# Last output tiles of three down projections: one tile by token halves instead of two, and the next stage's weight splits moved forward

## The chip, the cores and the metric

One core of a Trainium2 chip runs the whole program. The metric is the device time of one execution in microseconds (us); the kernel before takes 2347.71 us (median of 3 runs, 2346.6 to 2347.77).

## What is computed

Two streams of 256 tokens each (the latents `x` and a context `ctx`, width 1024) go through two layers in fp32. A layer is: feed-forward 1, a mixer (convolution, mLSTM, differential attention), feed-forward 2. Each of the three adds its gated result to the stream and normalizes:

```python
def post_norm(h, delta, g, b):
    return layer_norm(ALPHA * h + delta, g, b)

def modulate(h, shift, scale):
    return h * (1.0 + scale) + shift

def swiglu(u, w_up, w_down):
    a, v = jnp.split(u @ w_up, 2, axis=-1)
    return (jax.nn.silu(a) * v) @ w_down

# feed-forward 1 of a layer; the context stream does the same with mods_c
h = post_norm(h, 0.5 * mods[2] * swiglu(modulate(h, mods[0], mods[1]), ffn1_up[l], ffn1_down[l]),
              ln_g[l, 0], ln_b[l, 0])
```

`w_down` is 2816 x 1024. In the last layer the context stream is needed only until the mixer.

## The kernel before

**Layout.** Activations lie transposed: a [128, 8, 512] tensor `h` holds 8 tiles of 128 channels, and 512 tokens on the free axis, context first (columns 0 to 255), latents second (256 to 511). Every fp32 product is made of three fp32r matmuls: weights are split into `w_hi` (rounded, by ScalarE) and `w_lo` (the rest, by VectorE), activations into `u_hi` and `u_lo` in the same way, and `chunk` (lines 1091 to 1107) issues hi x hi, hi x lo and lo x hi for each block of 128 input channels, on lines 1101, 1102 and 1103. These three lines carry most of the kernel.

**Weights.** A chunk is a [128, up to 1024] piece of weights, loaded by SyncE into one of two `raw` slots, split by ScalarE (line 1618), then by VectorE (line 2350) into one of four slots of `w_hi`/`w_lo`. `ahead(base, c, i, 8)` on both engines splits the chunk that comes four after chunk c. The raw slot can be loaded again only when VectorE has finished the split from it two chunks earlier, and a `w_hi` slot can be written only when TensorE has used what lies in it. The order of work on every engine is written out by hand; engines meet at semaphores alone.

**A down projection** (`down` on TensorE, ScalarE and VectorE) computes 8 output tiles, two in a pass of 8 chunks: chunks q = 0 to 3 make the even tile (22 blocks of input channels in all), q = 4 to 7 the odd one. The first three passes (tiles 0 to 5) use all 512 tokens in each matmul. The last pass (i = 3, tiles 6 and 7) prepares the norm. In three of the four down projections both streams are alive: norms n = 1, 3 and 4 (feed-forward 1 and 2 of layer 0, feed-forward 1 of layer 1). There `seg_order(n)` gives a first and a second half of tokens (context then latents; for n = 4 latents then context). TensorE runs tile 6 and tile 7 for the first half (132 matmuls of 256 columns, counted by `half_done`), then both again for the second half (132 more, counted by `chunk_used`, into banks `LAST_DOWN`). So tile 6's four `w_hi` slots are read until the second half. Tile 7's weights lie apart (`APART`: in `apart_hi` and in idle columns of `u_hi`), so that the four slots can take the first chunks of the next stage as soon as tile 6 lets go of them.

**The norm.** It is taken apart so that it fits beside these matmuls:
- `pivot` (TensorE, line 1127, after q = 0), `pivot_out` (ScalarE) and `centre` (VectorE, line 2527) take the mean of tiles 0 to 5 off;
- `late_branch` (VectorE, line 2558) adds a late tile from PSUM; `squares` (ScalarE, line 1734) and `add_squares` (line 2538) sum the squares, `add_rest` (line 2547) the rest of the sum. `full_tiles(n)` says up to which tile this is done for both halves at once;
- `statistics` (TensorE, lines 1138 to 1143) sums over channels; `variance`, `deviation` (ScalarE, line 1745) and `inverse` follow; `spread` (TensorE, line 1171) broadcasts the result;
- `take_mean` (line 2580) and `scaled` (line 2589) finish the norm on VectorE, `modulate` (ScalarE, lines 1690 and 1692: two instructions for each tile) makes the next stage's input in full and rounded, `low_half` (line 2500) its rest. This goes by five items: tiles 0, 1, 2-3, 4-5, 6-7.

The next stage begins with `interleaved` (TensorE, lines 1174 to 1206): four chunks side by side, tile by tile of their input, first half of tokens first. Step k needs `u_ready` of tile k. Chunks 0 and 1 start at step 0, chunk 2 at step 2, chunk 3 at step 4. After step 2 it issues the second half's `statistics`, after step 4 its `spread`, and waits there for VectorE.

Of the kernel before, what the change touches and what calls it, by code (L numbers as in the profile page):

```python
# [87 lines left out]
def is_wo(n):  # L88
    return n % 3 == 2


def seg_order(n):

    if n >= 5:
        return [LAT]
    return [LAT, CTX] if n == 4 else [CTX, LAT]
# [4 lines left out]


def full_tiles(n):
    return 4 if is_wo(n) else 6


def branch_index(n, k, order):
# [13 lines left out]
def before(n, count, first=1):  # L121

    return sum(count(m) for m in range(first, n))


def halves_done(n):

    return before(n + 1, lambda m: (4 if is_wo(m) else 8) * (len(seg_order(m)) - 1))


def sums_before(n):
# [267 lines left out]
def build(nc, x, c, ctx, c_ctx, w_ada, b_ada, ln_g, ln_b, ffn1_up, ffn1_down, ffn2_up, ffn2_down,  # L399
# [211 lines left out]
    LAST_DOWN = (4, 5)  # L611
# [402 lines left out]
    def _(pe):  # L1014
# [287 lines left out]
        def down(layer, f):  # L1302
            base, a0, d0 = BASES[layer, f"down{f}"]
            t = slice(t0_of(layer) if f else 0, TOK)
            n = 3 * layer + 2 * f + 1

            if n == DEFERRED + 1:
                pe.wait_ge(up_moved, CH_UP - 2)
            else:
                pe.wait_ge(evac_act, a0 - 1)  # L1310
                pe.wait_ge(evac_dve, d0 - 1)

            block = ADA_OF.get((layer, f"down{f}"))

            def part(q, i, cols_of, signal=chunk_used, bank=None, after_k=None, then=None):
                r = base + q + 8 * i
                ks = (LAST_K if is_apart(r) else DOWN_K)[q % 4]
                if i in PAIRED.get(n, ()):
                    paired_chunk(r, (base + q) % SPLIT, q // 4, ks, q % 4 == 0, q % 4 == 3)
                    return  # L1320
                chunk(r, (base + q) % SPLIT, q // 4 if bank is None else bank, of(g_hi, g_lo, ks, cols_of), cols_of,
                      first=(q % 4 == 0), last=(q % 4 == 3), signal=signal, after_k=after_k, then=then)

            def body(i):
                for q in range(8):
                    if isinstance(i, int) and i == 0 and q < 4:

                        pe.wait_ge(g_ready, KF * (2 * layer + f) + DOWN_K[q][-1] + 1)
                    if q % 4 == 0 and not (n == DEFERRED + 1 and isinstance(i, int) and i == 0):

                        pe.wait_ge(evac_dve, d0 - 1 + 2 * i + q // 4)
                    part(q, i, t)
                    if q == 1 and block is not None and isinstance(i, int) and 0 < i <= ADA_DOWN[layer]:
                        ada_columns(block + i - 1)
            body(0)
            body(1)
            body(2)
            i = DOWN_BODIES - 1
            segs = seg_order(n)
            pe.wait_ge(evac_dve, d0 - 1 + 2 * i)  # L1340
            if len(segs) == 2:
                for q in range(8):
                    if q == 4:
                        pe.wait_ge(evac_dve, d0 - 1 + 2 * i + 1)
                    part(q, i, segs[0][1], half_done)
                    if q == 0:
                        pivot(n)
                    if q == 1 and block is not None and i <= ADA_DOWN[layer]:
                        ada_columns(block + i - 1)
                if block is not None:  # L1350
                    pe.wait_ge(ada_ev, block + ADA_DOWN[layer])
                part(0, i, segs[1][1], bank=LAST_DOWN[0], after_k=4, then=lambda: statistics(n, 0))
                part(1, i, segs[1][1], bank=LAST_DOWN[0], after_k=3, then=lambda: spread(n, 0))
                for q in range(2, 8):
                    part(q, i, segs[1][1], bank=LAST_DOWN[q // 4])
            else:
                for q in range(4):
                    part(q, i, t)
                    if q == 0:
                        pivot(n)  # L1360
                pe.wait_ge(evac_dve, d0 - 1 + 2 * i + 1)
                for q in range(4, 8):
                    part(q, i, segs[0][1], bank=LAST_DOWN[1])
                turn_out(range(0, 6))
                last_statistics(n)
                turn_out(range(6, KD))
# [233 lines left out]
    def _(act):  # L1600
# [141 lines left out]
        def deviation(n, order):  # L1742

            act.wait_ge(ln_var, segs_before(n) + order + 1)
            act.activation(stat[:, order, 4:6], stat[:, order, 2:4], ACT.Sqrt, bias=small[:, 0:1]).then_inc(ln_std, 1)
# [66 lines left out]
        def down(layer, f):  # L1812
            base = BASES[layer, f"down{f}"][0]
# [20 lines left out]
            if not two:  # L1834
# [4 lines left out]
                scale_tiles(n, (7,))  # L1839
                deviation(n, 0)  # L1840
                return
            squares(n, (6, 7))
            if two:
                deviation(n, 0)
                ahead(base, 4, i, 8)
                modulate(n, 0, (0,))
                ahead(base, 5, i, 8)
                modulate(n, 0, (1,))
                ahead(base, 6, i, 8)
                squares(n, (6,), 1)  # L1850
                modulate(n, 0, (2, 3))
                ahead(base, 7, i, 8)
                modulate(n, 0, (4, 5))
                squares(n, (7,), 1)
                modulate(n, 0, (6,))
                deviation(n, 1)
                modulate(n, 0, (7,))
                for k in range(KD):
                    modulate(n, 1, (k,))
                    if n == 4 and k in FIRST_AFTER:  # L1860
                        proj(layer, ("mq", FIRST_AFTER.index(k)))
                if f:
                    silu_table()
# [463 lines left out]
    def _(dve):  # L2327
# [443 lines left out]
        def down(layer, f):  # L2771
# [35 lines left out]
            ahead(base, 3, i, 8, down_kn(3, two))  # L2807
            add_squares(n, (5,))
            if two:
                dve.wait_ge(half_done, halves_done(n) - 4)  # L2810
                late_branch(n, 6, 0, 0)
                add_squares(n, (6,), 0)
                dve.wait_ge(half_done, halves_done(n))
                late_branch(n, 7, 1, 0)
                add_rest(n, 7, 0)
# [4 lines left out]
                after(taken)  # L2820
                scaled(n, 0, 0)
                scaled(n, 0, 1)
                ahead(base, 4, i, 8)
                low_half(n, 0, 0)
                taken = take_mean(n, 0, 4, KD)
                ahead(base, 5, i, 8)
                low_half(n, 0, 1)
                dve.wait_ge(chunk_used, base + 8 * i + 4)
                late_branch(n, 6, LAST_DOWN[0], 1)
                scaled(n, 0, 2)  # L2830
                ahead(base, 6, i, 8)
                add_squares(n, (6,), 1)
                after(taken)
                scaled(n, 0, 3)
                low_half(n, 0, 2)
                scaled(n, 0, 4)
                ahead(base, 7, i, 8)
                low_half(n, 0, 3)
                dve.wait_ge(chunk_used, base + 8 * i + 8)
                late_branch(n, 7, LAST_DOWN[1], 1)  # L2840
                add_rest(n, 7, 1)
                add_squares(n, (7,), 1)
                variance(n, 1)
# [571 lines left out]
```

## Time and profile before

| what | value |
|---|---|
| device time, median of 3 | 2347.71 us (2346.6 to 2347.77) |
| profiled execution | span 2345.9 us, from the first to the last instruction; the runs' median is 1.8 us above it |
| TensorE busy | 2324.3 us (99%), 12926 matmuls |
| VectorE busy | 1658.6 us (71%) |
| ScalarE busy | 1034.5 us (44%) |
| DMA | 356.89 MB, mean 152 GB/s |

A matmul's own duration in the profile covers its run through the array, and matmuls overlap, so the time that one costs in a stream is the distance from its start to the next one's. An engine's idle time counts only where TensorE later waits for it.

### The profile page before, as it was taken

The page shows a single profiled execution, that of the slowest core. Times are in us where ns is not written, and L with a number is a line of the kernel's source. Part 1 is how long each engine was busy: PE and PEld are TensorE (multiplying, and loading weights), DVE is VectorE, ACT ScalarE, POOL GpSimd, SP SyncE. Part 2 cuts the span into 40 slices and gives each one's busy share as a digit, 9 for nine tenths or more (in the row PEclk, how much of TensorE's full clock was granted, in tenths as well). Part 3 has the DMA queues.
Part 4 walks back from the last instruction along what each step waited for, and adds up shares of the span by engine and source line. Part 5 has one row for each costly group of instructions (what it writes and reads, how often), then busy time and mean ns, then how long its engine had stood idle before and what let it go on. Part 6 is the DMA issues. An engine that isn't in the chain of part 4 may idle for free.

```text
span 2345.9 us, 35713 instructions
## 1 busy us (share of the span) xinstructions
PE 2324.3 (99%) x12926; PEld 2024.5 (86%) x12926; DVE 1658.6 (71%) x2777; ACT 1034.5 (44%) x1765; POOL 194.4 (8%) x186
## 2 busy tenths in 40 slices
PE   8999999999999999999999999999999999999998
PEld 6888889888888888898888898888898898999997
DVE  6998577457757655669885368886665757878876
ACT  5423224435556544363222264322245347756554
POOL 2111000000000000021120000111100000001220
PEclk9999999999999999999999999999999999999999
DMA  8788465232222322338783328776544433656654
GB/s 276 241 249 246 127 213 149 82 95 76 73 68 81 95 81 70 110 91 254 237 246 113 94 80 249 232 237 181 180 117 117 117 99 103 172 143 196 193 160 141
DMA packets 540057, 356.89 MB, mean 152 GB/s; under 512 B 15206, under 2 KB 490896, under 8 KB 539920
## 3 DMA queue, kind: packets, MB, share of 16 engines
q1 hardware_dynamic: 538472, 354.70, 51.6%
q8 instruction: 84, 1.38, 0.3%
q10 hardware_dynamic: 1448, 0.38, 0.1%
q14 instruction: 53, 0.43, 0.1%
HBM read 337.20 MB, written 17.83 MB: 151 GB/s over the span
## 4 chain that ended last, share of the span: by engine, by line
PE 94%; DVE 2%; ACT 1%; issue 1%; DMA 1%; POOL 0%; DVEq 0%; SPq 0%; ACTq 0%; POOLq 0%
PE ps L1101 25%; PE ps L1103 25%; PE ps L1102 25%; PE ps L1401 2%; PE ps L1402 2%; PE ps L1400 2%; PE ps L1114 1%; PE ps L1475 1%; PE ps L1193 1%; PE ps L1195 1%; PE ps L1194 1%; PE ps L1512 1%; PE ps L1116 1%; DVE w_lo L2350 0%; PE ps L1413 0%
## 5 line engine op out<-in xcount | busy, mean ns | idle before, releaser
L1618 ACT ACTIVATE w_hi<-raw 128x1024 fp32r<-128x1024 f32 (+3 forms) x430 | 423.3, 985 | 848.9 <-PE ps L1103 661.1
L2350 DVE TENSOR_TENSOR w_lo<-raw,w_hi 128x1024 fp32r<-128x1024 f32 (+3 forms) x430 | 495.0, 1152 | 423.1 <-ACT w_hi L1618 417.6
L1101 PE MATMUL ps<-u_hi,w_hi 128*128 128x512 f32 (+2 forms) x2176 | 778.1, 358 | 1.1 <-DVE w_lo L2350 0.7
L1103 PE MATMUL ps<-u_hi,w_lo 128*128 128x512 f32 (+2 forms) x2176 | 773.5, 355 | 0.0
L1102 PE MATMUL ps<-u_lo,w_hi 128*128 128x512 f32 (+2 forms) x2176 | 773.1, 355 | 0.0
L1101 PEld LDWEIGHTS ps<-u_hi,w_hi 128*128 128x128 f32 x2176 | 411.2, 189 | 60.1 <-issue 1.3
L1103 PEld LDWEIGHTS ps<-u_hi,w_lo 128*128 128x128 f32 x2176 | 411.1, 189 | 57.7
L1102 PEld LDWEIGHTS ps<-u_lo,w_hi 128*128 128x128 f32 x2176 | 411.4, 189 | 55.8
L2768 DVE SCALAR_TENSOR_TENSOR ada_acc<-ada_in_up,cs,ada_acc 128x512 f32<-128x512 f32 x378 | 284.2, 813 | 0.0
L1101 PE MATMUL ps<-g,w_hi 128*128 128x512 f32 (+1 forms) x572 | 206.9, 362 | 0.0
L1102 PE MATMUL ps<-g,w_hi 128*128 128x512 f32 (+1 forms) x572 | 204.1, 357 | 0.0
L1103 PE MATMUL ps<-g,w_lo 128*128 128x512 f32 (+1 forms) x572 | 204.1, 357 | 0.0
L2282 POOL TENSOR_TENSOR fold<-fold 128x512 f32<-128x512 f32 x64 | 87.6, 1368 | 880.3 <-DMA fold<-fold_out 877.8
L1802 ACT ACTIVATE g<-scr 128x512 f32 (+1 forms) x66 | 41.8, 633 | 200.9 <-DVE scr L2678 192.1
L1101 PEld LDWEIGHTS ps<-g,w_hi 128*128 128x128 f32 x572 | 108.1, 189 | 16.8 <-DVE w_lo L2350 0.5
L1102 PEld LDWEIGHTS ps<-g,w_hi 128*128 128x128 f32 x572 | 108.1, 189 | 16.1 <-issue 0.7
L1103 PEld LDWEIGHTS ps<-g,w_lo 128*128 128x128 f32 x572 | 108.1, 189 | 15.5
L2350 DVE TENSOR_TENSOR w_lo<-h,w_hi 128x1024 fp32r<-128x1024 f32 (+2 forms) x66 | 71.6, 1087 | 18.9 <-ACT w_hi L1618 18.5
L2260 POOL TENSOR_TENSOR scr<-h 128x256 f32<-128x256 f32 x3 | 3.7, 1227 | 972.5 <-DVE h L2558 972.5
L1618 ACT ACTIVATE w_hi<-h 128x1024 fp32r<-128x1024 f32 (+2 forms) x66 | 62.0, 942 | 40.2 <-PE ps L1103 30.0
L1402 PE MATMUL ps<-w_lo,u_hi 128*128 128x512 f32 x192 | 74.8, 389 | 0.0
L1400 PE MATMUL ps<-w_hi,u_hi 128*128 128x512 f32 x192 | 74.8, 389 | 0.0
(394 smaller groups left out, 3678.0 us busy)
## 6 DMA issues: line engine op xcount, KB each, us to landing
raw<-in_ffn_up SPq DMA_DIRECT2D x150, 512.0 KB, 4.8
raw<-in_w_in SPq DMA_DIRECT2D x132, 512.0 KB, 3.8
ada_in_up<-in_w_ada SPq DMA_DIRECT2D x108, 512.0 KB, 4.6
raw<-in_ffn_down SPq DMA_DIRECT2D x67, 384.0 KB, 3.6
fold_out<-ada_acc SPq DMA_DIRECT2D x32, 512.0 KB, 3.5
fold<-fold_out SPq DMA_DIRECT2D x32, 512.0 KB, 5.4
raw<-in_ffn_down SPq DMA_DIRECT2D x42, 320.0 KB, 3.2
h<-in_ffn_up SPq DMA_DIRECT2D x22, 512.0 KB, 4.0
```

Source lines behind the costliest of these rows:

```text
L1101: pe.matmul(ps[bank][:, cols_of], wh, a_hi, start=a, stop=False)
L1102: pe.matmul(ps[bank][:, cols_of], wh, a_lo, start=False, stop=False)
L1103: m = pe.matmul(ps[bank][:, cols_of], wl, a_hi, start=False, stop=b)
L1114: pe.matmul(ps[bank][:, :].rearrange("p (s t) -> p s t", s=2), wh, g[:, :, k, SEG:TOK], start=(first and n == 0), stop=False)
L1400: pe.matmul(ps[t][:, :], u_hi[:, k, own], wh, start=(k == 0), stop=False)
L1401: pe.matmul(ps[t][:, :], u_lo[:, k, own], wh, start=False, stop=False)
L1402: m = pe.matmul(ps[t][:, :], u_hi[:, k, own], wl, start=False, stop=(k == KD - 1))
L1618: act.activation(hi, whole, ACT.Copy).then_inc(hi_done, 1)
L1802: act.activation(g_hi[:, 2 * i + q // 2, t0:TOK], scr[2 + q // 2][:, t0:TOK], ACT.Copy).then_inc(g_hi_done, 1)
L2282: pool.tensor_tensor(fold[:, 0:n, :], fold[:, 0:n, :], fold[:, n:2 * n, :], ALU.add).then_inc(fold_half, 1)
L2350: dve.tensor_tensor(lo, whole, hi.bitcast(F32), ALU.subtract).then_inc(lo_done, 1)
L2768: dve.scalar_tensor_tensor(ada_acc[:, s, :], w, by, ada_acc[:, s, :], ALU.mult, ALU.add).then_inc(ada_mul, 1)
```

## The change

Tile 6 is now computed for all tokens at once, like tiles 0 to 5; only tile 7 is done by halves. `full_tiles` of a down projection goes from 6 to 7, so tile 6's evacuation, squares and sums are done once for 512 columns. The first half's `statistics` and `spread` move from the second half of tile 6 to the second half of tile 7. The splits of the next stage's first four chunks (`ahead(base, 4..7, i, 8)`) move forward in the order of ScalarE and VectorE.

```diff
 def full_tiles(n):
-    return 4 if is_wo(n) else 6
+    return 4 if is_wo(n) else 7
...
-    return before(n + 1, lambda m: (4 if is_wo(m) else 8) * (len(seg_order(m)) - 1))
+    return before(n + 1, lambda m: 4 * (len(seg_order(m)) - 1))
...
                 for q in range(8):
                     if q == 4:
                         pe.wait_ge(evac_dve, d0 - 1 + 2 * i + 1)
-                    part(q, i, segs[0][1], half_done)
+                    if q < 4:
+                        part(q, i, t)
+                    else:
+                        part(q, i, segs[0][1], half_done)
...
-                part(0, i, segs[1][1], bank=LAST_DOWN[0], after_k=4, then=lambda: statistics(n, 0))
-                part(1, i, segs[1][1], bank=LAST_DOWN[0], after_k=3, then=lambda: spread(n, 0))
-                for q in range(2, 8):
-                    part(q, i, segs[1][1], bank=LAST_DOWN[q // 4])
+                part(4, i, segs[1][1], bank=LAST_DOWN[1])
+                part(5, i, segs[1][1], bank=LAST_DOWN[1], after_k=0, then=lambda: statistics(n, 0))
+                part(6, i, segs[1][1], bank=LAST_DOWN[1], after_k=1, then=lambda: spread(n, 0))
+                part(7, i, segs[1][1], bank=LAST_DOWN[1])
...
-            squares(n, (6, 7))
             if two:
+                ahead(base, 4, i, 8)
+                squares(n, (6,))
+                ahead(base, 5, i, 8)
+                squares(n, (7,))
                 deviation(n, 0)
-                ahead(base, 4, i, 8)
-                modulate(n, 0, (0,))
-                ahead(base, 5, i, 8)
-                modulate(n, 0, (1,))
                 ahead(base, 6, i, 8)
-                squares(n, (6,), 1)
+                modulate(n, 0, (0, 1))
+                ahead(base, 7, i, 8)
                 modulate(n, 0, (2, 3))
-                ahead(base, 7, i, 8)
+                squares(n, (7,), 1)
                 modulate(n, 0, (4, 5))
-                squares(n, (7,), 1)
-                modulate(n, 0, (6,))
                 deviation(n, 1)
-                modulate(n, 0, (7,))
+                modulate(n, 0, (6, 7))
...
             if two:
-                dve.wait_ge(half_done, halves_done(n) - 4)
+                dve.wait_ge(chunk_used, base + 8 * i + 4)
                 late_branch(n, 6, 0, 0)
+                ahead(base, 4, i, 8)
                 add_squares(n, (6,), 0)
+                ahead(base, 5, i, 8)
                 dve.wait_ge(half_done, halves_done(n))
                 late_branch(n, 7, 1, 0)
...
                 scaled(n, 0, 0)
                 scaled(n, 0, 1)
-                ahead(base, 4, i, 8)
+                ahead(base, 6, i, 8)
                 low_half(n, 0, 0)
                 taken = take_mean(n, 0, 4, KD)
-                ahead(base, 5, i, 8)
+                scaled(n, 0, 2)
                 low_half(n, 0, 1)
-                dve.wait_ge(chunk_used, base + 8 * i + 4)
-                late_branch(n, 6, LAST_DOWN[0], 1)
-                scaled(n, 0, 2)
-                ahead(base, 6, i, 8)
-                add_squares(n, (6,), 1)
+                ahead(base, 7, i, 8)
                 after(taken)
                 scaled(n, 0, 3)
                 low_half(n, 0, 2)
                 scaled(n, 0, 4)
-                ahead(base, 7, i, 8)
-                low_half(n, 0, 3)
                 dve.wait_ge(chunk_used, base + 8 * i + 8)
                 late_branch(n, 7, LAST_DOWN[1], 1)
+                low_half(n, 0, 3)
                 add_rest(n, 7, 1)
```

VectorE between the first half's spread and the second half's sums, in the kernel before (L2589 scales a tile or two, L2350 splits a chunk of the next stage, L2500 is the low half of the next input, L2580 takes the mean off, L2558 adds a late tile, L2538 adds squares):

```order
L2589 TENSOR_TENSOR h<-h,ps 128x256 x2
L2350 TENSOR_TENSOR w_lo<-raw,w_hi 128x1024
L2500 TENSOR_TENSOR u_lo<-scr_82,u_hi 128x256
L2580 TENSOR_TENSOR h<-h,ps 128x4x256
L2350 TENSOR_TENSOR w_lo<-raw,w_hi 128x1024
L2500 TENSOR_TENSOR u_lo<-scr_82,u_hi 128x256
L2558 SCALAR_TENSOR_TENSOR h<-ps,gate,h 128x256
L2589 TENSOR_TENSOR h<-h,ps 128x2x256
L2350 TENSOR_TENSOR w_lo<-raw,w_hi 128x1024
L2538 TENSOR_TENSOR scr_80<-scr_80,scr_79 128x256
```

The same place in the changed kernel (each line number is one higher):

```order
L2590 TENSOR_TENSOR h<-h,ps 128x256 x2
L2351 TENSOR_TENSOR w_lo<-raw,w_hi 128x1024
L2501 TENSOR_TENSOR u_lo<-scr_82,u_hi 128x256
L2581 TENSOR_TENSOR h<-h,ps 128x4x256
L2590 TENSOR_TENSOR h<-h,ps 128x2x256
L2501 TENSOR_TENSOR u_lo<-scr_82,u_hi 128x256
L2351 TENSOR_TENSOR w_lo<-raw,w_hi 128x1024
L2590 TENSOR_TENSOR h<-h,ps 128x2x256
L2501 TENSOR_TENSOR u_lo<-scr_78,u_hi 128x2x256
L2590 TENSOR_TENSOR h<-h,ps 128x2x256
L2559 SCALAR_TENSOR_TENSOR h<-ps,gate,h 128x256
L2501 TENSOR_TENSOR u_lo<-scr_82,u_hi 128x2x256
```

Two of the four splits and the second half's share of tile 6 are gone from here. What follows is the second half's L2548 and L2539 (sum and squares of tile 7), which now stand behind the low half of tiles 4-5.

ScalarE around the second half's square of tile 7 (L1734), before (L1690 and L1692 are the two instructions of `modulate`, here for tiles 4, 5 and 6, L1618 is a split):

```order
L1618 ACTIVATE w_hi<-raw 128x1024
L1690 ACTIVATE scr_82<-h,mod_b,mod_a 128x256
L1692 ACTIVATE u_hi<-h,mod_b,mod_a 128x256
L1690 ACTIVATE scr_82<-h,mod_b,mod_a 128x256
L1692 ACTIVATE u_hi<-h,mod_b,mod_a 128x256
L1734 ACTIVATE scr_79<-h 128x256
L1690 ACTIVATE scr_78<-h,mod_b,mod_a 128x256
```

And in the changed kernel (tiles 3, 4 and 5; L1737 is the square):

```order
L1693 ACTIVATE scr_78<-h,mod_b,mod_a 128x256
L1695 ACTIVATE u_hi<-h,mod_b,mod_a 128x256
L1737 ACTIVATE scr_79<-h 128x256
L1693 ACTIVATE scr_82<-h,mod_b,mod_a 128x256
L1695 ACTIVATE u_hi<-h,mod_b,mod_a 128x256
L1693 ACTIVATE scr_82<-h,mod_b,mod_a 128x256
L1695 ACTIVATE u_hi<-h,mod_b,mod_a 128x256
```

The square of tile 7 now stands ahead of tiles 4 and 5, so ScalarE waits for VectorE's L2559 before it begins them.

## Rows read from the trace of the kernel before

**Rows 1.** The page, busy time of each engine: us, share of the span, instructions.
```profile
PE 2324.3 (99%) x12926; PEld 2024.5 (86%) x12926; DVE 1658.6 (71%) x2777; ACT 1034.5 (44%) x1765; POOL 194.4 (8%) x186
```

**Rows 2.** Timeline of PE, n = 3: start us, duration us, line; 512 columns, 60 steps.
```profile
1335.62 0.39 PE L1101 MATMUL ps<-g,w_hi 128*128 128x512 f32 x1
...
1349.22 0.28 PE L1101 MATMUL ps<-g,w_hi 128*128 128x256 f32 x1
```

**Rows 3.** Timeline of PE, n = 3: pivot, then 126 steps of 256 columns.
```profile
1351.38 1.02 PE L1127 MATMUL ps<-scr,con 128*128 128x512 f32 x2
1351.84 0.68 PE L1101 MATMUL ps<-g,w_hi 128*128 128x256 f32 x1
...
1352.47 0.28 PE L1103 MATMUL ps<-g,w_lo 128*128 128x256 f32 x1
...
1367.59 0.28 PE L1103 MATMUL ps<-g,w_lo 128*128 128x256 f32 x1
```

**Rows 4.** Timeline of PE, n = 3: first statistics, first spread.
```profile
1367.70 0.50 PE L1138 MATMUL ps<-con,scr 128*128 128x1 f32 x4
...
1370.82 0.60 PE L1171 MATMUL ps<-con,stat 128*128 128x128 f32 x4
```

**Rows 5.** Timeline of PE, n = 3: next stage's first matmul, second statistics.
```profile
1383.49 0.28 PE L1193 MATMUL ps<-u_hi,w_hi 128*128 128x256 f32 x1
...
1386.01 0.50 PE L1138 MATMUL ps<-con,scr 128*128 128x1 f32 x4
```

**Rows 6.** Timeline of DVE, n = 3, after the first spread.
```profile
1371.53 0.75 DVE L2589 TENSOR_TENSOR h<-h,ps 128x256 f32<-128x256 f32 x2 [0.62 <-PE ps L1171]
1372.20 1.22 DVE L2350 TENSOR_TENSOR w_lo<-raw,w_hi 128x1024 fp32r<-128x1024 f32 x1
1373.33 0.42 DVE L2500 TENSOR_TENSOR u_lo<-scr,u_hi 128x256 fp32r<-128x256 f32 x1
1373.67 1.22 DVE L2580 TENSOR_TENSOR h<-h,ps 128x1024 f32<-128x1024 f32 x1
...
1375.93 0.42 DVE L2500 TENSOR_TENSOR u_lo<-scr,u_hi 128x256 fp32r<-128x256 f32 x1
1376.27 0.48 DVE L2558 SCALAR_TENSOR_TENSOR h<-ps,gate,h 128x256 f32<-128x256 f32 x1
1376.66 0.68 DVE L2589 TENSOR_TENSOR h<-h,ps 128x512 f32<-128x512 f32 x1
...
1380.57 0.69 DVE L2500 TENSOR_TENSOR u_lo<-scr,u_hi 128x512 fp32r<-128x512 f32 x1
```

**Rows 7.** Timeline of DVE, n = 3: tile 7 of the second half, its sum and squares.
```profile
1384.10 0.48 DVE L2558 SCALAR_TENSOR_TENSOR h<-ps,gate,h 128x256 f32<-128x256 f32 x1
1384.61 0.42 DVE L2547 TENSOR_TENSOR scr<-h 128x256 f32<-128x256 f32 x1
1385.06 0.42 DVE L2538 TENSOR_TENSOR scr<-scr,scr 128x256 f32<-128x256 f32 x1
```

**Rows 8.** Timeline of ACT, n = 3: modulation of two tiles, then the square.
```profile
1381.39 0.59 ACT L1690 ACTIVATE scr<-h,mod_b,mod_a 128x256 f32<-128x256 f32 x1
1381.88 0.59 ACT L1692 ACTIVATE u_hi<-h,mod_b,mod_a 128x256 fp32r<-128x256 f32 x1
...
1384.61 0.42 ACT L1734 ACTIVATE scr<-h 128x256 f32<-128x256 f32 x1 [1.15 <-DVE h L2558]
```

**Rows 9.** Timeline of PE, n = 1: a wait in the last pass, and the matmul before it.
```profile
385.83 0.28 PE L1103 MATMUL ps<-g,u_lo 128*128 128x256 f32 x1
386.52 0.39 PE L1101 MATMUL ps<-g,u_hi 128*128 128x256 f32 x1 [0.41 <-DVE u_lo L2350]
```

**Rows 10.** Windows of PE at the kernel's end: us, PE busy (instructions), granted clock, DMA.
```profile
2336.50:2337.50 1.00, 1.00 (x9) 1.00 0.00 0
2337.60:2340.30 2.70, 0.00 (x0) 1.00 0.00 0
2340.50:2342.50 2.00, 0.00 (x0) 0.50 0.35 131
```

## The prediction

> **What bounds the kernel now.** The page's first part comes first: TensorE (PE in rows) is busy for 2324.3 of 2345.9 us, 99% [rows 1]. VectorE (DVE) at 71% and ScalarE (ACT) at 44% have room on average, so every us that the change moves counts only through TensorE: matmul time saved, or a wait of TensorE that was not there. The next view is the timeline of TensorE in the last pass of a down projection. I work in the stage of n = 3, where nothing else goes on, and count t from the first matmul of that pass, 1349.22 us [rows 2]. Statistics start at t = 18.48 and the spread at 21.60 [rows 4], the next stage's first matmul at 34.27 and the second statistics at 36.79 [rows 5], all with no wait of TensorE. That they have none is a matter of cover: between the first spread and the next stage TensorE has 12.7 us of matmuls, under which the first half's normalizing is done. The timelines of DVE and ACT [rows 6 to 8] show how long that work is. VectorE's low half of tile 0 is there at t = 24.5, that of tile 1 at 27.1, that of tiles 2-3 at 32.0 [rows 6], where TensorE wants them at 34.3, 35.0 and 35.7.
>
> **What is taken off TensorE.** Tile 6 takes 66 matmuls of 512 columns in place of 132 of 256. A step of 512 columns is (1349.22 - 1335.62) / 60 = 0.2267 us [rows 2], one of 256 is (1367.59 - 1352.47) / 126 = 0.120 us [rows 3]. That is 66 x (0.240 - 0.2267) = 0.88 us for a stage, 2.6 us for the three. The Trainium skill, in "TensorE: Matmul & The Clock Gate", section "Back-to-back issue gap", gives N / 2.4 + 2.5 ns for a lone matmul of N columns at the full clock; by that a pair of 256 costs only 2.5 ns more than one of 512, and the gain would be 0.2 us a stage. The rows decide, with 13 ns.
> In n = 1 TensorE also waits 0.41 us for a split of tile 7's weights [rows 9]. The first half of tile 7 now starts some 7 us later (66 x 0.2267 against 66 x 0.12), so this wait goes, with the late restart after it: 0.5 us.
>
> **What the change moves.** It halves the cover. Of the second half's matmuls only tile 7's 66 are left, and the first half's statistics and spread stand inside them. Step by step, in t:
> - tile 6 whole 14.96, plus the pivot's 0.86 (from 1351.38 to 1352.47 less two steps [rows 3]): 15.82. The first half of tile 7, 7.92: 23.74.
> - 21 matmuls, 2.52: statistics at 26.26. They cost 1.32 (3.12 between the rows less 15 steps) [rows 4]. VectorE has added tile 7 and its squares by then: it needs three instructions and a square, 1.7 us.
> - 21 matmuls more: spread at 30.10, which costs 0.43. 24 matmuls are left, 2.88: the next stage at 33.41, where 34.27 was. Cover after the spread: 3.3 us instead of 12.7.
> VectorE starts `scaled` 0.71 us after the spread does [rows 4, 6], at 30.81. With the starts of neighbouring rows as the length of each [rows 6]:
> - two small `scaled` 0.67, a split 1.13, low half of tile 0: done at 33.03, 0.4 before TensorE needs it. No wait, just.
> - mean off tiles 4 to 7 1.13, `scaled` of tiles 2-3 0.60, low half of tile 1: done at 35.1. TensorE wants it at 33.41 + 6 x 0.12 = 34.13: **1.0 us** of wait.
> - a split 1.13, `scaled` of 4-5 0.60, low half of tiles 2-3 0.69: done at 37.55, ScalarE's four instructions for them (0.49 each [rows 8]) being ready at 36.9. TensorE has step 1 done at 36.0: **1.6 us**.
> - TensorE's step 2 (9 matmuls) ends at 38.85, and it comes to the second half's statistics. These need VectorE's evacuation, sum and squares of tile 7, at 1384.10 to 1385.48 in rows 7, which before were done 0.5 us ahead of TensorE. Now the evacuation starts at 38.1, behind `scaled` of 6-7. Behind it the new order crosses the two engines: ScalarE's square of tile 7 stands ahead of its modulation of tiles 4 and 5, and VectorE's low half of 4-5 stands ahead of the sum and the squares. So the chain is evacuation 0.48, square 0.42, four modulations 2.0, low half 0.69, sum 0.35, squares 0.42: done at 42.4. **3.6 us**, the largest wait.
> A wait also makes TensorE's restart late: the first matmul after one lasts 0.39 instead of 0.28 us [rows 9]; I put 0.15 for each of the three. Sum of the waits: 1.0 + 1.6 + 3.6 + 0.45 = 6.65 us.
> Behind the statistics ScalarE does the deviation and then four modulations of tiles 6 and 7 (before, two of them were behind); the second half's mean and scaling come some 1 us later against TensorE. In n = 1 and 3 the second half of the interleaved chunks, in n = 4 the projection's next splits, wait for them. The trace has no row for that; nothing is the lower bound, 1.1 us (this delay and a restart) the upper, and I take 0.8, since these chains have less than a us to spare.
> The four early splits cost nothing: two now stand where VectorE waits for TensorE's half of tile 7 (t = 16 to 24), the cover being that wait. They do not repay the cost, since no wait of TensorE for a next-stage split is there to be removed in n = 3.
> Tile 6 done once saves VectorE and ScalarE an instruction or two, in the stretch before t = 16, where nothing is late. The last down projection (n = 6) has one half only and keeps its order.
>
> **The sum.** n = 3: 6.65 + 0.8 - 0.88 = 6.6 us. n = 4: the same. n = 1: 6.6 - 0.5 = 6.1. Together 19.3 us, 0.8%. The profiled execution's span is 2345.9 us, and the median of the runs stands 1.8 above a span; 2347.7 + 19.3 = **2367 us**. About 0.2% (4.7 us) is what a measurement of this kernel can tell from no change.
>
> **The rivals.**
> *The clock falls too.* TensorE's granted clock is full (2.4 GHz) for the whole working part. At the end TensorE is idle from about 2337.5; until 2340.3 the clock is still full, from 2340.5 on it is half (1.2 GHz) [rows 10]. So some 2.9 us of idleness brought it down, and my third wait has 3.6, with two short ones just before. Against: before that end TensorE had only small matmuls, in my stage it is dense. Were it to fall in each stage for some 5 us of dense matmuls, each would lose 2.5 us: 2367 + 7.5 = 2374.5 us. Below, a fall that ends with the wait costs nothing. The Trainium skill's page named above, section "What's actually happening", calls the lower clock the state of an idle engine, which activity releases; by that rule too a long wait is paid for twice. Chance 30%.
> *Only the early waits cost.* If the crossed chain is shorter than I make it, by ScalarE getting to the square sooner or TensorE being later there, the third wait shrinks by 2.5 us: 2367 - 7.5 = 2359.5 us. For it: 3.6 is the difference of two long sums. Against: every link is a row. Chance 15%.
> *The cover still holds (the other side).* Then the change is worth 3 x 0.88 + 0.5 = 3.1 us: 2344.6 us, faster. It decides itself at one place, VectorE must have tiles 0 to 3 ready by the end of step 1, at 33.41 + 1.44 = 34.85, which is 4.0 us from its first `scaled`. Before, that took it from 1371.53 to 1381.26 [rows 6]; without the tile 6 work and the wait for a load it is still 6.6 us of its own instructions. For it speaks only that the splits of chunks 0 and 1 are out of the way. Chance 4%.
> *It lands within the measure*, waits of less than 2 us a stage: 1%.
>
> **How the numbers follow.** Forecast 50%, clock 30%, early waits only 15%, cover holds 4%, same 1%. The range takes in the clock case and the short case with their bounds: 2359 to 2376 us, which leaves out the rest and the far ends. Faster by over 0.2%: 0.04. Within: 0.01. Slower: 0.95.
>
> **What would show it.** In the changed profile, TensorE's idle time before L1193 (one higher in the new numbering) should hold waits for `u_lo` of about 1.0 and 1.6 us three times each, and the second L1138 waits of about 3.6 us, released by VectorE's squares or sum; TensorE's matmul count falls by 198. The next stage's first matmul comes 0.9 us sooner after the pass's first. The granted clock around those waits tells the first rival. I am wrong if the low halves of tiles 1 and 2-3 end before TensorE's steps, or if the second statistics follow step 2 without a gap.

## The result and the profile after

The changed kernel takes **2372.03 us** (median of 4 runs, 2370.02 to 2372.4) where the kernel before takes 2347.36 (4 runs, 2346.6 to 2347.77): a ratio of 1.0104, interval 1.0092 to 1.0116. It is slower, inside the range, 5 us above the predicted time. The spans say the same, 2370.6 against 2345.9 us.

The page of the changed kernel, busy time of each engine (answers to [rows 1]):

```profile
PE 2334.2 (98%) x12728; PEld 2022.5 (85%) x12728; DVE 1659.7 (70%) x2774; ACT 1033.9 (44%) x1762; POOL 196.7 (8%) x186
```

TensorE runs 198 matmuls fewer and is busy 9.9 us longer. A count that falls while busy time rises means that matmuls became slower somewhere; the windows further down show where. The table of TensorE's waits (us in total, times, longest) holds the rest:

```profile
PE ps L1193 <- DVE u_lo L2501: 7.5, 7, 1.5
PE ps L1138 <- DVE scr L2548: 7.4, 3, 2.8
```

Neither group had more than 0.3 us before. Timeline of TensorE in n = 3 (start, duration, line, and in brackets the idle time before it with its releaser), from the pivot on; answers to [rows 3, 4, 5]:

```profile
1360.52 1.02 PE L1127 MATMUL ps<-scr,con 128*128 128x512 f32 x2
...
1372.31 0.28 PE L1101 MATMUL ps<-g,apart_hi 128*128 128x256 f32 x1
...
1382.74 0.50 PE L1138 MATMUL ps<-con,scr 128*128 128x1 f32 x4
...
1386.57 0.60 PE L1171 MATMUL ps<-con,stat 128*128 128x128 f32 x4
...
1389.89 0.28 PE L1193 MATMUL ps<-u_hi,w_hi 128*128 128x256 f32 x1
...
1391.63 0.38 PE L1193 MATMUL ps<-u_hi,w_hi 128*128 128x256 f32 x1 [0.86 <-DVE u_lo L2501]
...
1394.13 0.39 PE L1193 MATMUL ps<-u_hi,w_hi 128*128 128x256 f32 x1 [1.53 <-DVE u_lo L2501]
...
1398.60 1.01 PE L1138 MATMUL ps<-con,scr 128*128 128x1 f32 x4 [2.84 <-DVE scr L2548]
```

The pivot comes after 18 steps of the pass, now of 512 columns, so the pass begins at 1360.52 - 18 x 0.2267 = 1356.44; that is t = 0. The next stage's first matmul is at t = 33.45 (33.41 predicted), then come three waits. The other two stages have the same three: 0.86, 1.52 and 2.40 us in n = 1; 0.86, 1.52 and 2.18 in n = 4. VectorE in the same stretch (answers to [rows 6, 7]):

```profile
1387.29 0.75 DVE L2590 TENSOR_TENSOR h<-h,ps 128x256 f32<-128x256 f32 x2 [1.34 <-PE ps L1171]
...
1391.15 0.42 DVE L2501 TENSOR_TENSOR u_lo<-scr,u_hi 128x256 fp32r<-128x256 f32 x1
...
1393.38 0.69 DVE L2501 TENSOR_TENSOR u_lo<-scr,u_hi 128x512 fp32r<-128x512 f32 x1
...
1394.59 0.47 DVE L2559 SCALAR_TENSOR_TENSOR h<-ps,gate,h 128x256 f32<-128x256 f32 x1
1397.51 0.69 DVE L2501 TENSOR_TENSOR u_lo<-scr,u_hi 128x512 fp32r<-128x512 f32 x1 [2.45 <-ACT u_hi L1695]
1398.12 0.42 DVE L2548 TENSOR_TENSOR scr<-h 128x256 f32<-128x256 f32 x1
1398.46 0.42 DVE L2539 TENSOR_TENSOR scr<-scr,scr 128x256 f32<-128x256 f32 x1
```

and ScalarE, which those 2.45 us wait for:

```profile
1395.10 0.42 ACT L1737 ACTIVATE scr<-h 128x256 f32<-128x256 f32 x1 [1.75 <-DVE h L2559]
1395.42 0.58 ACT L1693 ACTIVATE scr<-h,mod_b,mod_a 128x256 f32<-128x256 f32 x1
...
1396.90 0.58 ACT L1695 ACTIVATE u_hi<-h,mod_b,mod_a 128x256 fp32r<-128x256 f32 x1
```

This is the crossed chain: VectorE's evacuation at 1394.59, ScalarE's square, its four modulations, VectorE's low half at 1397.51, and only then the sum that TensorE's second statistics wait for. ScalarE waits 1.75 us for VectorE's evacuation, and VectorE then 2.45 us for ScalarE's last modulation. The windows of TensorE over the same stretch (us, PE busy and instructions, granted clock, DMA share, GB/s) hold what the prediction's sum did not:

```profile
1386.00:1394.90 8.90, 6.51 (x53) 1.00 0.37 87
1395.00:1405.20 10.20, 7.36 (x33) 0.50 0.11 32
1405.30:1414.00 8.70, 8.70 (x75) 1.00 0.02 4
```

For 10.24 us (1394.97 to 1405.21 in the clock's record) the granted clock is 0.50, the 1.2 GHz level. It falls 0.8 us after the end of the second wait, before the third begins, and comes back 6.6 us after the third is over. n = 1 (from 408.52) and n = 4 (from 1770.44) have a low stretch of 10.24 us too; there it begins within 0.3 us of the second wait's end (408.22, 1770.71). In the kernel before, the clock is full from 15.9 to 2340.4 us. At the low level a step of 256 columns starts every 0.214 us instead of 0.12:

```profile
1401.54 0.41 PE L1194 MATMUL ps<-u_lo,w_hi 128*128 128x256 f32 x1
1401.75 0.41 PE L1195 MATMUL ps<-u_hi,w_lo 128*128 128x256 f32 x1
```

So several accounts were open. **A:** there are two costs, the three waits and the fall of the clock that they bring. **B:** the fall is free, since it lies in waits that VectorE sets anyway. The opposite of B was open too: the low clock is nearly all of the cost, and waits of this size would be cheap without it. And within the waits: which of the change's parts made them, the halved cover or the order of the work?

### The profile page after: what moved, and what is told of

The parts are those of the page before. It is cut to its first block, busy times and chain, and to the rows that moved or that the text cites. A ratio compares the mean times of both kernels' runs of the same rounds, so it can differ in the third digit from the quotient of the medians.

```text
span 2370.6 us, 35302 instructions
## 1 busy us (share of the span) xinstructions
PE 2334.2 (98%) x12728; PEld 2022.5 (85%) x12728; DVE 1659.7 (70%) x2774; ACT 1033.9 (44%) x1762; POOL 196.7 (8%) x186
## 4 chain that ended last, share of the span: by engine, by line
PE 92%; DVE 3%; ACT 2%; issue 2%; DMA 1%; POOL 0%; DVEq 0%; SPq 0%; ACTq 0%; POOLq 0%
PE ps L1101 25%; PE ps L1103 25%; PE ps L1102 25%; PE ps L1405 2%; PE ps L1404 2%; PE ps L1403 2%; PE ps L1114 1%; PE ps L1193 1%; PE ps L1195 1%; PE ps L1194 1%; DVE w_lo L2351 1%; PE ps L1478 1%; PE ps L1515 1%; DMA raw<-in_w_in 1%; PE ps L1116 1%
## 5 line engine op out<-in xcount | busy, mean ns | idle before, releaser
L2769 DVE SCALAR_TENSOR_TENSOR ada_acc<-ada_in_up,cs,ada_acc 128x512 f32<-128x512 f32 x378 | 290.8, 830 | 0.9 <-DMA ada_in_up<-in_w_ada 0.8
L1101 PE MATMUL ps<-g,w_hi 128*128 128x512 f32 (+1 forms) x506 | 194.3, 384 | 0.0
L1103 PE MATMUL ps<-g,w_lo 128*128 128x512 f32 (+1 forms) x506 | 192.3, 380 | 0.0
L1102 PE MATMUL ps<-g,w_hi 128*128 128x512 f32 (+1 forms) x506 | 192.3, 380 | 0.0
L1101 PEld LDWEIGHTS ps<-g,w_hi 128*128 128x128 f32 x506 | 95.2, 188 | 19.0 <-issue 0.7
L1102 PEld LDWEIGHTS ps<-g,w_hi 128*128 128x128 f32 x506 | 95.2, 188 | 18.5 <-issue 0.7
L1103 PEld LDWEIGHTS ps<-g,w_lo 128*128 128x128 f32 x506 | 95.2, 188 | 18.2
L1193 PE MATMUL ps<-u_hi,w_hi 128*128 128x256 f32 x224 | 68.8, 307 | 7.8 <-DVE u_lo L2501 7.5
```

The lines of the kernel that those rows point to most:

```text
L1101: pe.matmul(ps[bank][:, cols_of], wh, a_hi, start=a, stop=False)
L1102: pe.matmul(ps[bank][:, cols_of], wh, a_lo, start=False, stop=False)
L1103: m = pe.matmul(ps[bank][:, cols_of], wl, a_hi, start=False, stop=b)
L1193: pe.matmul(ps[q][:, own], wh, u_hi[:, k, own], start=(k == 0), stop=False)
L2769: dve.scalar_tensor_tensor(ada_acc[:, s, :], w, by, ada_acc[:, s, :], ALU.mult, ALU.add).then_inc(ada_mul, 1)
```

## The experiments

Each kernel ran beside the kernel before on the same chip. The first four stand against 2347.61 us (7 runs, 2346.33 to 2348.73), the last three against 2347.17 (21 runs, 2346.46 to 2347.84).

**1. Waits without the clock (fill).** TensorE multiplies something of no use into a free bank ahead of each of the three waits, so that it is busy in most of the time in which it would wait; what the kernel computes stays the same.

```diff
+        def filler(base, seg, count):
+            for _ in range(count):
+                pe.matmul(ps[4][:, seg], w_hi[:, base % SPLIT, 0:P], u_hi[:, 0, seg], start=True, stop=True)
...
                     if q == 0:
+                        if n and not is_wo(n) and nth in (1, 2):
+                            filler(base, orders[0][1], (6, 12)[nth - 1])
                         pe.wait_ge(u_ready, u_count(n, order, k))
...
+                        if not is_wo(n):
+                            filler(base, orders[0][1], 23)
                         statistics(n, 1)
```

> The changed kernel with filler on TensorE: ahead of each of its three waits at the start of the next stage it repeats one matmul of 256 columns into the unused bank 4, 6, 12 and 23 times (0.7, 1.4 and 2.8 us at the full clock, a little less than the waits of 1.0, 1.7 and 3.6 us). Theory A (two costs: the waits, and the fall of the clock that they bring): the waits' ends stay where VectorE sets them, the granted clock stays 1.00 over the span, and the time falls by what the clock cost, some 3 us a stage, to 2362 to 2365 us. Rival B (the clock's fall is free, since it lies in a wait that VectorE sets anyway): the clock stays up, but the time stays at 2371 to 2373 us.

Measured: **2365.64 us** (2365.31 to 2366.27), ratio 1.0078 (1.0061 to 1.0095), span 2363.9. The windows of TensorE in n = 3:

```profile
1386.00:1394.90 8.90, 8.66 (x71) 1.00 0.48 125
1395.00:1405.20 10.20, 9.82 (x81) 1.00 0.01 2
```

and its second statistics and a wait in the second half (for tile 2):

```profile
1396.52 0.61 PE L1138 MATMUL ps<-con,scr 128*128 128x1 f32 x4 [0.38 <-DVE scr L2557]
...
1408.85 0.39 PE L1200 MATMUL ps<-u_hi,w_hi 128*128 128x256 f32 x1 [0.30 <-DVE u_lo L2510]
```

The clock stays full to the kernel's end. The second statistics stand at t = 1396.52 - (1358.44 - 4.08) = 42.16, exactly where they stand in the changed kernel (1398.60 - 1356.44 = 42.16): what they wait for has not moved, only TensorE's clock is full when it comes. The clock is thus worth 2372.0 - 2365.6 = 6.4 us, 2.1 a stage, and the waits and the rest 18.3 us. That is A. B would have left the time at 2371 to 2373 us, and a kernel whose loss was nearly all clock would have come back close to the 2347 of the kernel before. A's own number, 2362 to 2365 us, was missed by 0.6, and the trace says why. From the second statistics to the second spread the changed kernel needs 6.94 us (1398.60 to 1405.54), this one 3.94 (to 1400.46): 3.0 us for the clock, as expected. But this kernel now reaches the second half's matmuls before their input is ready, and waits twice there, for tile 0 (below) and for tile 2 (above):

```profile
1405.09 0.28 PE L1202 MATMUL ps<-u_hi,w_lo 128*128 128x256 f32 x1
1405.42 0.39 PE L1200 MATMUL ps<-u_hi,w_hi 128*128 128x256 f32 x1
```

These two waits cost 0.86 us with their restarts in n = 1 and in n = 3. The changed kernel, later by then, has neither.

**2. The chain uncrossed (uncross).** Tile 7's sum and squares ahead of the low half of tiles 4 and 5 on VectorE; nothing else.

```diff
                 late_branch(n, 7, LAST_DOWN[1], 1)
-                low_half(n, 0, 3)
                 add_rest(n, 7, 1)
                 add_squares(n, (7,), 1)
+                low_half(n, 0, 3)
```

> The changed kernel with one edit on VectorE: the sum and the squares of tile 7's second half stand ahead of the low half of tiles 4-5, so that they no longer wait for ScalarE's four modulations. Theory A (the third wait is the crossed chain): the wait before the second statistics shrinks from 2.2 to 2.8 us to under 0.8; but the work behind comes late too, so a new wait of about 1.3 us for the second half's tile 0 opens in n = 1 and 3, and the gain is 1.5 to 3 us a stage: 2363 to 2368 us. If the first two waits alone bring the clock down, it still falls in each stage for 10.24 us. Rival C (the third wait is what brings the clock down): the clock stays up, and 3 us a stage more are gained: 2358 to 2361 us.

Measured: **2361.74 us** (2361.35 to 2362.77), ratio 1.0062 (1.0045 to 1.0079). Timeline of TensorE in n = 3:

```profile
1388.21 0.39 PE L1193 MATMUL ps<-u_hi,w_hi 128*128 128x256 f32 x1 [0.86 <-DVE u_lo L2501]
1390.71 0.58 PE L1193 MATMUL ps<-u_hi,w_hi 128*128 128x256 f32 x1 [1.52 <-DVE u_lo L2501]
1392.79 0.85 PE L1138 MATMUL ps<-con,scr 128*128 128x1 f32 x4
```

The third wait is gone (0.12 us are left in n = 4) and the first two are untouched, so the crossing made the third. Taking it away is worth 10.3 us of the 24.7, the shorter low stretches that come with it included: the clock fell all the same, as the window after the second wait shows, but for 6.83, 6.83 and 3.41 us instead of 10.24 each:

```profile
1390.70:1397.30 6.60, 6.59 (x29) 0.50 0.27 76
```

So 0.86 and 1.52 us of idleness, a us apart, bring the clock down here without any longer wait. Part of the gain comes back as a new wait in n = 4, where the second half's work is now later:

```profile
1791.52 0.47 PE L1101 MATMUL ps<-u_hi,w_hi 128*128 128x512 f32 x1 [1.25 <-DVE w_lo L2351]
```

The expectation was right on the cause and wrong on two other points. The time is 1.3 us below its 2363 to 2368, and the wait of 1.3 us that it put into the second half of n = 1 and n = 3 isn't there: neither stage has any wait after the second statistics. Rival C, by which the clock stays up, is out.

**3. The splits back (late).** The order of tile 6 and 7 as changed, but the four early splits on ScalarE and VectorE about where the kernel before has them. VectorE's part (ScalarE's goes with it, each split behind one item):

```diff
                 late_branch(n, 6, 0, 0)
-                ahead(base, 4, i, 8)
                 add_squares(n, (6,), 0)
-                ahead(base, 5, i, 8)
...
                 scaled(n, 0, 1)
-                ahead(base, 6, i, 8)
+                ahead(base, 4, i, 8)
                 low_half(n, 0, 0)
                 taken = take_mean(n, 0, 4, KD)
+                ahead(base, 5, i, 8)
+                low_half(n, 0, 1)
                 scaled(n, 0, 2)
-                low_half(n, 0, 1)
-                ahead(base, 7, i, 8)
+                ahead(base, 6, i, 8)
...
                 scaled(n, 0, 4)
+                ahead(base, 7, i, 8)
```

> The changed kernel with the splits of the next stage's four chunks back at their old places in the orders of ScalarE and VectorE, after the first spread. Theory A (VectorE's own work after the spread sets the waits, so each split of 1.13 us put back there lengthens them, and the loads behind the raw slots come later too): about 3.9 us a stage more waiting, 2380 to 2386 us. Rival D (the early splits buy nothing, since they stand where nobody waits): within 2 us of the changed kernel, 2370 to 2374 us.

Measured: **2383.39 us** (2383.13 to 2383.9), ratio 1.0154 (1.0137 to 1.0171), the slowest of all. TensorE in n = 3:

```profile
1394.83 0.39 PE L1193 MATMUL ps<-u_hi,w_hi 128*128 128x256 f32 x1 [1.42 <-DVE w_lo L2352]
1399.81 0.58 PE L1193 MATMUL ps<-u_hi,w_hi 128*128 128x256 f32 x1 [3.65 <-DVE u_lo L2502]
1405.41 1.02 PE L1138 MATMUL ps<-con,scr 128*128 128x1 f32 x4 [3.31 <-DVE scr L2549]
```

The early splits repay 11.4 us, 3.8 a stage, as expected. That number holds longer low stretches too, 13.65 us in each stage instead of 10.24. The part of the change that looks like an extra is what keeps the other part from costing half as much again.

**4. Only the merging undone (cols256).** Tile 6 keeps its new place, but each 512-column matmul is two of 256, the second into another bank.

```diff
+                    for bank, own in ((0, slice(0, SEG)), (2, slice(SEG, TOK))):
...
+                        pe.matmul(ps[bank][:, own], wh, g_hi[:, k, own], start=a, stop=False)
+                        pe.matmul(ps[bank][:, own], wh, g_lo[:, k, own], start=False, stop=False)
+                        m = pe.matmul(ps[bank][:, own], wl, g_hi[:, k, own], start=False, stop=b)
```

> The changed kernel, but tile 6 is computed in matmuls of 256 columns again, both halves right behind one another (second half in bank 2). All else is as in the changed kernel. This measures what the merging of the halves itself is worth. By the steps of the trace (0.120 and 0.2267 us): 3 x 0.88 = 2.6 us slower than the changed kernel, 2374 to 2375.5 us. By N / 2.4 + 2.5 ns: 0.5 us slower, 2372 to 2373 us.

Measured: **2373.32 us** (2372.56 to 2374.09), ratio 1.011 (1.0094 to 1.0127); 1.3 us above the changed kernel, which is between the two ranges expected. The two also differ in their low stretches (here 10.24, 10.24 and 6.83 us), so the times don't isolate the merging. The clean reading is inside the pass, where nothing waits: from the pivot to tile 7's first matmul,

```profile
1361.36 1.02 PE L1127 MATMUL ps<-scr,con 128*128 128x512 f32 x2
...
1373.72 0.28 PE L1101 MATMUL ps<-g,apart_hi 128*128 128x256 f32 x1
```

are 12.36 us against 11.79 in the changed kernel, over 48 pairs: 12 ns a pair. That is near the 13 ns of the prediction and far from 2.5.

**5. Only the first statistics and spread earlier (early).** The first half's statistics stand 3 matmuls earlier in tile 7's second half, its spread 18. It widens the cover of the first two waits and leaves the crossed chain alone.

```diff
-                part(4, i, segs[1][1], bank=LAST_DOWN[1])
-                part(5, i, segs[1][1], bank=LAST_DOWN[1], after_k=0, then=lambda: statistics(n, 0))
-                part(6, i, segs[1][1], bank=LAST_DOWN[1], after_k=1, then=lambda: spread(n, 0))
+                part(4, i, segs[1][1], bank=LAST_DOWN[1], after_k=5, then=lambda: statistics(n, 0))
+                part(5, i, segs[1][1], bank=LAST_DOWN[1], after_k=1, then=lambda: spread(n, 0))
+                part(6, i, segs[1][1], bank=LAST_DOWN[1])
```

> The changed kernel with one edit on TensorE: the first statistics come after 6 instead of 7 blocks of tile 7's second half, the first spread after 8 instead of 14, so that 2 us more cover stands behind the spread. Theory A: the first wait goes, the second shrinks from 1.7 to about 0.6 us, the third stays at 3.6 us at the full clock: 1.7 us a stage, 2365 to 2368 us, if the third wait alone also brings the clock down. If only the first two did that, the clock stays up: 2360 to 2362 us.

Measured: **2365.88 us** (2364.35 to 2367.65), ratio 1.0078 (1.0063 to 1.0093). TensorE in n = 3:

```profile
1390.95 0.39 PE L1193 MATMUL ps<-u_hi,w_hi 128*128 128x256 f32 x1 [0.78 <-DVE u_lo L2501]
1395.42 1.01 PE L1138 MATMUL ps<-con,scr 128*128 128x1 f32 x4 [3.14 <-DVE scr L2548]
```

The first wait is gone, the second halved, the third is longer, because TensorE reaches it sooner and at full clock. The clock falls inside the third wait this time, at 1394.08, for 6.83 us (in n = 4 inside it too, in n = 1 0.4 us after its end). The time is as expected for a clock that the third wait also brings down. Together with uncross: the two short waits bring it down without the long one, and the long one after a single short one does too.

**6. All three waits taken away by order alone (mend).** As early, and: the next stage's third split ahead of the variance; the first three groups of tiles scaled at once; the second statistics and spread one step later; tile 7's second half added before the low half of tiles 2-3; the chain uncrossed; the second half's first mean taken before the low half of tiles 6-7 (below the lines shown). ScalarE's and TensorE's parts follow it. VectorE's part, which carries most:

```diff
+                ahead(base, 6, i, 8)
                 variance(n, 0)
...
-                scaled(n, 0, 0)
-                scaled(n, 0, 1)
-                ahead(base, 6, i, 8)
-                low_half(n, 0, 0)
+                for item in (0, 1, 2):
+                    scaled(n, 0, item)
                 taken = take_mean(n, 0, 4, KD)
-                scaled(n, 0, 2)
-                low_half(n, 0, 1)
+                low_half(n, 0, 0)
                 ahead(base, 7, i, 8)
                 after(taken)
                 scaled(n, 0, 3)
-                low_half(n, 0, 2)
-                scaled(n, 0, 4)
+                low_half(n, 0, 1)
                 dve.wait_ge(chunk_used, base + 8 * i + 8)
                 late_branch(n, 7, LAST_DOWN[1], 1)
-                low_half(n, 0, 3)
+                low_half(n, 0, 2)
+                scaled(n, 0, 4)
                 add_rest(n, 7, 1)
                 add_squares(n, (7,), 1)
+                low_half(n, 0, 3)
```

> Tile 6 whole, as in the changed kernel, with the cover as short as there, but a new order around it: first statistics 1 block and first spread 5 blocks of channels earlier, second statistics and spread one step later in the next stage, the third early split ahead of the variance, the three first items scaled at once, sum and squares of tile 7's second half ahead of the low half of tiles 4-5. Theory A (the waits come from where the work stands, and can be ordered away): at most 0.4 us of wait a stage, no fall of the clock, 0.5 us a stage gained against the kernel before and 0.5 more in n = 1: 2344.5 to 2347 us, so 0.02 to 0.12% faster than before. Rival E (half the cover can't hold the first half's norm whatever the order): waits of 2 us and more a stage, 2354 us and above.

Measured: **2345.78 us** (11 runs, 2344.97 to 2346.62), ratio 0.9995 (0.9985 to 1.0004). The windows of TensorE in n = 3 are full, at full clock:

```profile
1380.00:1388.00 8.00, 8.00 (x67) 1.00 0.56 139
1388.00:1396.00 8.00, 8.00 (x68) 1.00 0.01 3
```

and the waits around the first half's norm have shrunk to one of 0.17 us, in n = 4:

```profile
1743.22 0.71 PE L1171 MATMUL ps<-con,stat 128*128 128x128 f32 x4 [0.17 <-DVE stat L2573]
```

The low halves are just in time. Timeline of VectorE (first `scaled`, then the low halves of tile 1 and tiles 2-3) and of TensorE (first spread, next stage's first matmul):

```profile
1376.38 1.35 DVE L2589 TENSOR_TENSOR h<-h,ps 128x256 f32<-128x256 f32 x3
...
1380.85 0.41 DVE L2500 TENSOR_TENSOR u_lo<-scr,u_hi 128x256 fp32r<-128x256 f32 x1
1381.18 0.47 DVE L2558 SCALAR_TENSOR_TENSOR h<-ps,gate,h 128x256 f32<-128x256 f32 x1
1381.58 0.68 DVE L2500 TENSOR_TENSOR u_lo<-scr,u_hi 128x512 fp32r<-128x512 f32 x1
```

```profile
1375.27 0.71 PE L1171 MATMUL ps<-con,stat 128*128 128x128 f32 x4
...
1380.85 0.28 PE L1193 MATMUL ps<-u_hi,w_hi 128*128 128x256 f32 x1
```

Tile 1 is done when the next instruction starts, at 1381.18, and wanted at 1380.85 + 6 x 0.12 = 1381.57; tiles 2-3 are done at 1382.18 and wanted at 1382.29. With half the cover the work fits, with 0.1 us to spare. The gain is 1.4 us in medians, against an interval that just reaches 1: the fastest version found, but not one that this measurement tells from the kernel before. The expectation (2344.5 to 2347 us) holds, and rival E, by which half the cover can't hold the norm in any order, is out.

**7. What the merging is worth once nothing waits (mend256).** Mend, with tile 6 in 256 columns as in cols256.

> The reordered kernel with tile 6 in matmuls of 256 columns (both halves right behind one another). No clock falls in either, so this is the clean measure of merging: by the trace's steps 2.6 us above the reordered kernel (2.4 us by the 12.1 ns a pair that the last pair of profiles gave), by N / 2.4 + 2.5 ns 0.5 us above it.

Measured: **2347.23 us** (11 runs, 2346.73 to 2347.87), ratio 1.0001 (0.9992 to 1.001). Merging is worth 1.45 us in medians where TensorE has no waits, between the 2.6 and the 0.5 expected (all 11 runs without it are above all 11 with it); worked out, it is 198 pairs x 12 ns = 2.4. The two profiled spans, 2345.8 and 2343.3, differ by 2.5, but mend's profiled execution is its second fastest and mend256's its second slowest, so that number is in part chance. Where the missing us of the 2.4 went isn't shown.

## Why the prediction came out right, and which step was short

The measured 24.7 us are 18.3 of waits and what hangs on them, where the sum had 19.3, and 6.4 of clock, where the sum had nothing. The range held the result because it took in the rival.

- **Which views.** Right. The busy shares (VectorE 71%) gave no hint of trouble; the 12.7 us of cover between [rows 4] and [rows 5] did.
- **The first two waits.** 1.0 and 1.6 us predicted with the restart apart; measured 0.86 and 1.53. Tile 1's low half was put at t = 35.1, tiles 2-3 at 37.55; they ended at 35.05 (1391.49, the next instruction's start) and 37.55 (1393.99). Adding starts of neighbouring rows works.
- **The third wait.** 3.6 us predicted, 2.84 measured (2.40 and 2.18 in the other stages). The releasing chain was right: done at t = 42.4 predicted, the statistics start at 42.16. TensorE's own arrival was wrong: put at 38.85, it came at 1395.76, t = 39.3, because the clock had fallen. Early, where it comes at full clock, has 3.14.
- **The clock.** This is the step that failed. The sum priced it at nothing, and the rival gave it 30% and 7.5 us. It fell in all three stages and cost 6.4 us (fill): 2.1 a stage where the rival had 2.5. The argument against it, that my stage is dense, did not hold: between the first two waits stand only 1.0 us of dense matmuls (1391.63 to 1392.60), and the fall came in every stage before the third wait. The rival's number, 2374.5, is nearer to 2372.0 than the forecast's 2367. Its condition, 2.9 us of idleness, was read from [rows 10]; here 2.4 us in two pieces were enough. The Trainium skill's page "TensorE: Matmul & The Clock Gate", section "What's actually happening", which the rival named, says that activity releases the lower clock. The trace agrees in direction (the clock comes back under dense matmuls, at 1405.21), and the waits were paid for twice, by a third more.
- **The merging.** 13 ns a pair predicted from [rows 2, 3], 12 measured. The 2.5 ns of the Trainium skill's page "TensorE: Matmul & The Clock Gate", section "Back-to-back issue gap", would make 0.5 us of three stages; mend against mend256 shows 1.45.
- **The second half's 0.8 us a stage.** Right at the full clock: fill loses 0.86 us in the second half of n = 1 and of n = 3. In the changed kernel the low clock covers it; there is no wait of TensorE in the second half of these stages. This is why the clock's 3.0 us in n = 3 show as 2.1 in the time. In n = 4 the projection's split is late by 0.29 us in the changed kernel, as before the change.
- **The stages.** Fill is the changed kernel at full clock, so its stages compare with the sum. Its pivots come at 374.28, 1358.44 and 1732.88 us, those before at 372.46, 1351.38 and 1719.48; 1.9 us of each shift are the 18 wider steps ahead of a pivot. That makes 5.1, 6.3 and (to the end of the span) 6.5 us for n = 1, 3 and 4, where 6.1, 6.6 and 6.6 were predicted. In n = 3 it can be followed: the second statistics 5.4 us later in the pass than before the change (5.6 predicted), 0.1 for their restart (0.15), 0.86 behind them (0.8). The changed kernel has 7.2, 8.5 and 9.0. In n = 1 the wait of [rows 9] was worth 0.67 us (0.57 up to the start at 386.52, 0.10 up to the next at 386.74), not 0.5; the rest of what makes this stage a us cheaper than its sum isn't traced.
- **n = 1.** The 0.41 us wait of [rows 9] is gone, as said.
- **The early splits.** "They do not repay the cost" is right, but the prediction named no worth of theirs, though its own sum rests on two splits fewer behind the spread: without the early splits the change costs 36 us, not 25 (late).
- **Cover still holds.** Wrong for this order (4% given), but not impossible: mend shows that half the cover is enough once the order on VectorE is the one that TensorE asks for. I had put 6.6 us of VectorE's work against 4.0 us of time. In mend the work is 5.8 us (1376.38 to 1382.18) and the time longer, since the spread stands 2.1 us earlier against the pass.
- **Not tried:** whether fewer useless matmuls, or some at only one of the waits, keep the clock up; and which of mend's moves could be left out.

## What to carry to other kernels

When work for the next stage is hidden under one engine's last matmuls, measure that cover in us before moving anything out of it, and add up the other engines' starts against it: the busy shares say nothing of it. Where a value goes back and forth between two engines, an instruction that waits for the other engine must not stand ahead of the one whose result the bottleneck wants. And where a sum gives TensorE two or three waits close together, put the lower clock into the sum, not among the rivals: here it added a third to what the waits cost.

## What the runs showed that was not expected

The clock fell with no single wait over 1.53 us before it (in n = 3 0.86 and 1.53 us, the second beginning 1.0 us after the first's end), and stayed low through dense matmuls: 10.24 us in the changed kernel, 6.83 in early, 13.65 in late, whose waits are the longest (1.42, 3.65, 3.31). The low stretch isn't the same in every execution of a kernel: the mean granted clock of early's four runs goes from 0.994 to 0.996, and the fastest has 0.996. In the kernel before, a wait of 0.51 us, two of 0.41 and several of 0.3 never brought it down. Useless matmuls into a free bank, in a time in which TensorE would have waited, made the kernel 6.4 us faster.
